# A mixture-of-experts decoder kernel in which expert gate and up rows are interleaved and loaded as pairs

## The reference

```
def swiglu(h, wg, wu, wd):
    return (jax.nn.silu(h @ wg) * (h @ wu)) @ wd

def moe_swiglu(h, router_w, wg, wu, wd):
    logits = (h @ router_w).astype(jnp.float32)
    top_val, top_idx = lax.top_k(logits, TOP_K)
    top_w = jax.nn.softmax(top_val, axis=-1)
    gates = jnp.sum(jax.nn.one_hot(top_idx, N_EXPERTS, dtype=jnp.float32) * top_w[..., None], axis=-2).astype(h.dtype)
    y = jnp.zeros_like(h)
    for e in range(N_EXPERTS):
        y = y + gates[..., e:e + 1] * swiglu(h, wg[e], wu[e], wd[e])
    return y
```

## Time and profile before

| what | value |
|---|---|
| median of three runs | 1382.75 us (1382.27 to 1382.86) |
| span of the profiled execution, first to last instruction | 1382.1 us |
| PE busy | 1368.8 us, 99% of the span |
| DVE, ACT busy | 808.3 us, 661.5 us |
| moved by DMA | 454.9 MB, 329 GB/s over the span, about 430 GB/s from 620 us to 1370 us |
| TensorE clock granted, mean | 0.998 of full speed |

### The profile page before, as it was taken

One profiled execution on the slowest core, in us unless ns is written; L12 is line 12 of the kernel. 1 busy time (PEld: TensorE's weight loads), 2 busy tenths in 40 slices (PEclk: granted clock), 3 DMA queues, 4 the chain that ended last, 5 costly groups with the idle time before them and its releaser, 6 DMA issues.

```text
span 1382.1 us, 17732 instructions
## 1 busy us (share of the span) xinstructions
PE 1368.8 (99%) x6681; PEld 938.3 (68%) x6681; DVE 808.3 (58%) x1143; ACT 661.5 (48%) x886; POOL 10.3 (1%) x22
## 2 busy tenths in 40 slices
PE   8999999999999999999999999999999999999998
PEld 7887788888898877843434888534888534888532
DVE  5878666554557786631113989423889423989311
ACT  7657646444366575511002787312787302787210
POOL 2000000000000000000000000000000000000000
PEclk9999999999999999999999999999999999999999
DMA  9555446555544576899999999999999999999997
GB/s 354 191 177 184 152 136 231 183 183 184 182 153 155 181 264 269 309 403 429 429 433 427 430 431 428 429 432 428 429 430 423 399 431 427 430 429 430 428 430 295
DMA packets 84242, 454.90 MB, mean 329 GB/s; under 512 B 5624, under 2 KB 7936, under 8 KB 58048
## 3 DMA queue, kind: packets, MB, share of 16 engines
q1 hardware_dynamic: 83232, 452.47, 81.7%
q0 software_dynamic: 752, 1.23, 0.3%
q10 hardware_dynamic: 176, 0.07, 0.0%
HBM read 452.69 MB, written 1.06 MB: 328 GB/s over the span
## 4 chain that ended last, share of the span: by engine, by line
PE 92%; DVE 3%; ACT 3%; DMA 2%; issue 1%; DVEq 0%; ACTq 0%; SPq 0%
PE pA L837 39%; PE pB L837 19%; PE pB L1351 10%; PE pA L1351 8%; PE pA L1415 7%; PE pA L861 2%; DMA first_run<-expert_w_gate_dram 2%; PE pB L861 1%; DVE w_lo L1873 1%; PE pB L1249 1%; ACT w_hi L1514 1%; PE pA L1279 0%; PE pB L1069 0%; ACT early_hi L1514 0%; DMA aqk<-mix_norm_g_dram 0%
## 5 line engine op out<-in xcount | busy, mean ns | idle before, releaser
L1873 DVE TENSOR_TENSOR w_lo<-raw,w_hi 128x1024 fp32r<-128x1024 f32 x128 | 153.1, 1220 | 58.0 <-ACT w_hi L1514 57.6
L1873 DVE TENSOR_TENSOR w_lo<-first_run,w_hi 128x1024 fp32r<-128x1024 f32 x126 | 149.1, 1219 | 30.9 <-ACT w_hi L1514 29.6
L1514 ACT ACTIVATE w_hi<-raw 128x1024 fp32r<-128x1024 f32 x128 | 131.9, 1058 | 56.2 <-PE pB L837 32.2
L1873 DVE TENSOR_TENSOR w_lo<-late,w_hi 128x1024 fp32r<-128x1024 f32 x126 | 150.8, 1222 | 11.9 <-ACT w_hi L1514 3.6
L1514 ACT ACTIVATE w_hi<-first_run 128x1024 fp32r<-128x1024 f32 x126 | 130.9, 1065 | 52.0 <-DMA first_run<-expert_w_gate_dram 26.5
L1514 ACT ACTIVATE w_hi<-late 128x1024 fp32r<-128x1024 f32 x126 | 131.8, 1060 | 30.6 <-PE pA L837 15.1
L1824 ACT ACTIVATE ex_act<-pA 64x512 f32<-64x512 f32 x15 | 8.9, 591 | 242.0 <-PE pA L1351 194.4
L1873 DVE TENSOR_TENSOR early_lo<-raw,early_hi 128x1024 fp32r<-128x1024 f32 x58 | 69.8, 1221 | 34.3 <-ACT early_hi L1514 34.2
L2373 DVE TENSOR_TENSOR x<-pA,x 128x512 f32<-128x512 f32 x28 | 18.8, 688 | 118.2 <-PE pA L1280 116.9
L1351 PE MATMUL pB<-late,x_narrow 128*64 128x512 f32 x272 | 78.0, 592 | 0.0
L837 PE MATMUL pA<-w_hi,hT_hi 128*128 128x512 f32 x192 | 77.1, 402 | 0.0
(11 more groups left out here) (463 smaller groups left out, 2792.8 us busy)
## 6 DMA issues: line engine op xcount, KB each, us to landing
first_run<-expert_w_gate_dram SPq DMA_DIRECT2D x28, 1792.0 KB, 17.7
first_run<-expert_w_up_dram SPq DMA_DIRECT2D x28, 1792.0 KB, 15.3
late<-expert_w_gate_dram SPq DMA_DIRECT2D x28, 1792.0 KB, 15.5
late<-expert_w_up_dram SPq DMA_DIRECT2D x28, 1792.0 KB, 17.4
raw<-w_in_dram SPq DMA_DIRECT2D x43, 1024.0 KB, 5.1
first_run<-expert_w_down_dram SPq DMA_DIRECT2D x21, 2048.0 KB, 15.9
late<-expert_w_down_dram SPq DMA_DIRECT2D x28, 1024.0 KB, 17.6
late<-expert_w_down_dram SPq DMA_DIRECT2D x14, 2048.0 KB, 21.9
```

The costliest lines, as they stand in the source:

```text
L1514: f(like_raw(m, halves_slot(m)[0]), raw_slot(m), ACT.Copy).then_inc(s["w_hi_done"], 1)
L1873: tt(like_raw(m, lo), raw_slot(m), like_raw(m, hi.bitcast(F32)), ALU.subtract).then_inc(s["w_lo_done"], 1)
```

## The change

The function that launches the kernel joins the gate and up matrices along their last axis before the launch, so that in DRAM each gate line of 14,336 bytes is followed by the up line of the same number. A narrow job loads such a pair of rows at once: 28,672 bytes per partition, 3.67 MB, into the place of two rows. A wide job still loads single rows, which are now every other 14,336 bytes of the joined matrix. Job 0 also reads its pieces out of the joined matrix, in the same sizes as before.

```
     def wait_item(eng, narrow, kind, c, w):
-            at_pass, run, slot = item_at[narrow][kind, c]
-            if slot == RUN_ROWS:
+            at_pass, run, slot = item_at[narrow]["gate" if narrow and kind == "up" else kind, c]
+            if slot % 2 and slot < RUN_ROWS:
+                eng.wait_ge(row_loaded[run][slot], 16 * (1 if narrow else at_pass + 2) + 64 * w)
+            elif slot == RUN_ROWS:
...
-                gate, up, down = [w[0][bass.ds(e, 1)] for w in (expert_gate, expert_up, expert_down)]
-                gate, up = [w.rearrange("e (k p) n -> p (e k) n", p=P) for w in (gate, up)]
+                both, down = [w[0][bass.ds(e, 1)] for w in (expert_gate_up, expert_down)]
+                both = both.rearrange("e (k p) n -> p (e k) n", p=P)
+                gate, up = both[:, :, 0:ROW], both[:, :, ROW:]
...
                     for (kind, c, *n), at_pass, run, slot, at, size in items[is_narrow(j)]:
+                        if is_narrow(j) and kind == "up":
+                            continue
+                        if is_narrow(j) and kind == "gate":
+                            size = 2 * ROW
                         part_free(j, at_pass, run, at, size)
-                        if kind == "down":
+                        if is_narrow(j) and kind == "gate":
+                            src = both[:, c:c + 1, :]
+                        elif kind == "down":
...
+def rows_together(gate, up):
+    import numpy as np
+    return np.concatenate([gate, up], axis=3)
```

More of the change, by code:

```diff
@@ L166, in program @@
             q_norm_g, k_norm_g, w_branch_a, w_branch_b, w_out, ffn_norm_g, dense_gate, dense_up, dense_down,
-            router_w, expert_gate, expert_up, expert_down, consts, bucket_hot, bucket_mask, bias_rows, out):
+            router_w, expert_gate_up, expert_down, consts, bucket_hot, bucket_mask, bias_rows, out):
     with ExitStack() as ctx:
@@ L2513, in tables @@
     return c.reshape(P, 8 * P), hot, mask
+def rows_together(gate, up):
+    import numpy as np
+    return np.concatenate([gate, up], axis=3)
 _INS = ["x", "rel_bias", "mix_norm_g", "w_in", "conv_w", "conv_b", "igate_b", "fgate_b", "mlstm_norm_g",
         "q_norm_g", "k_norm_g", "w_branch_a", "w_branch_b", "w_out", "ffn_norm_g", "dense_w_gate", "dense_w_up",
-        "dense_w_down", "router_w", "expert_w_gate", "expert_w_up", "expert_w_down"]
+        "dense_w_down", "router_w", "expert_w_gate_up", "expert_w_down"]
 def kernel(**inputs):
@@ L2526 @@
     nc = bacc.Bacc("TRN2", target_bir_lowering=False, num_devices=1, dynamic_dma_scratch_size=4096)
+    inputs["expert_w_gate_up"] = rows_together(np.asarray(inputs["expert_w_gate"]), np.asarray(inputs["expert_w_up"]))
     arrays = {f"{n}_dram": np.ascontiguousarray(inputs[n]) for n in _INS}
```

## The result

| | before | after |
|---|---|---|
| median | 1382.8 us (1382.27 to 1383.39) | 1389.4 us (1386.95 to 1392.29) |
| ratio | 1 | 1.0043, 95% interval 1.0032 to 1.0055 |
| span of the profiled execution | 1382.1 us | 1388.2 us |

The account below looks back on a forecast made before the run. PE was taken to set the pace, hiding the loads. 1382.1 + 0 (loads) + 0 (issue) + 0 (gate rows) = 1382.1, and with 0.65 us from span to median 1382.7 us; range 1380.9 to 1386.0 us, 8 in 10.

Parts of the forecast that it names:

- What bounds the kernel: Whole kernel: PE sets the pace and the loads keep up, with 0.8 to 1.7 us to spare.
- four places where the loads could stop PE: Starts of first, second and third wide jobs and the last load: 0.95, 1.6, 0.84 and 1.7 us to spare.
- Fewer loads, longer rows: Narrow jobs from job 1: 32 pairs replace 64 loads, -0.3 us for the stream, zero for the total.
- Later issue: Pairs issued where up rows were: job 1 loses nothing, job 5 0 to 1.0 us, taken 0.5; total zero, worst 0.2.
- The upper bound: Lead needed by a load, at most 2.7 us: a 1 MB load landed after 5.1 us, 2.4 of it moving.
- loses nothing by either: Pair 4 of job 1, lead 2.9 us: no loss by the bounds of 1.5 and 2.7 us on the lead needed.
- pairs are issued too late: Narrow jobs: queue runs dry once per job; with a need of 5 us, 6.5 us slower, 1389.2 us; chance 0.10.
- Later landing of gate rows: Narrow jobs: PE's gate row waits for its up row too; nothing lost, smallest spare 1.5 us.
- the rest: Wide jobs' doubled row spacing, SP's extra address instruction per up load, job 0's pieces, unchanged engine order: zero cost.
- Faster, by an earlier start of the second wide job: PE's wait there is the loads' after all; up to 3.5 us gained, 1379.2 us; chance 0.08.
- Slower by instruction fetches behind longer rows: Four narrow jobs: some 11 fetches each wait 0.53 us for one row more; 5.8 us, 1388.5 us; chance 0.04.

Follow-up runs that it names:

- The kernel with the shorter stream: Changed kernel, but a narrow job's load of down unit 12 brings 64 numbers per partition instead of 2048, with wrong weights there: 1384.78 us, ratio 1.0010.
- the ample kernel: Changed kernel with pairs only for rows 1, 5, 6 and 7 of each narrow job, the other rows loaded singly: 1383.03 us, ratio 1.0003.
- the first kernel of loads alone: No computation, ten phases of 14 loads with varied row bytes and loads under way: 431 GB/s at 28,672 bytes and two, 356 at 10,240 and two.
- the last kernel: Loads only, 28,672-byte rows alternating with shorter ones, second half with extra rows on ScalarE's queue: at 4.25 to 4.3 us lead, mean loss 0.0, then 0.2 us.
- the layout alone: Changed kernel with the joined matrix kept, but narrow jobs loading single rows of 14,336 bytes, each with its own wait: 1384.19 us, ratio 1.0001.
- single rows issued late: Kernel before, with two matrices, but a narrow job's gate row also waits for the place of its up row: 1389.44 us, ratio 1.0039.
- the short kernel: Changed kernel with pairs only for rows 0, 2, 3 and 4 of each narrow job, the other rows loaded singly: 1390.07 us, ratio 1.0049.

## Why the prediction was wrong, point by point

*What bounds the kernel* was right: PE sets the pace, the loads have 0.8 to 1.7 us to spare at the starts of wide jobs and at the end, and "a gain in the loads is worth nothing; a loss beyond about 0.8 us is paid". The kernel with the shorter stream shows it from the other side. But its four places where the loads could stop PE left out the last up rows of wide jobs, where 0.73 and 1.51 us of the waits stand.

*Fewer loads, longer rows* was right: 433 GB/s for pairs at ample lead against 430 expected, worth nothing in the ample kernel. In these traces a fixed cost per load shows only on an idle queue. In the first kernel of loads alone, these two, issued at 288.89 and 582.07 us, were each the first of a phase (DMA view: size and us to landing):

```profile
place<-expert_w_gate_up_dram SPq DMA_DIRECT2D x1, 1792.0 KB, 7.1
...
place<-expert_w_gate_up_dram SPq DMA_DIRECT2D x1, 3584.0 KB, 11.0
```

That is 7.1 - 4.3 = 2.8 and 11.0 - 8.5 = 2.5 us beyond the moving. The Trainium skill's page "DMA: Bandwidth & Descriptors" (section "Anatomy of one DMA") gives about 2.0 us for the GpSimd path, near these two of SP's queue; for loads behind a queue with enough work, which came 8.5 us apart for 8.5 us of moving, the trace still disagrees.

*Later issue* is the step that failed. The issues came where it put them (670.77 and 680.65 us, against 670.87 and 680.75 for the up rows), and the leads were no shorter than it had worked out (3.5 us for pair 4 of job 1 where it said 2.9, 3.0 for pair 2 of job 5 where it said 1.7). It looked at these two pairs alone, and the second lost nothing; pair 3 of job 1, which it did not look at, lost 1.4 us. What failed is the bound on the lead that is needed: 1.5 to 2.7 us, where the runs show some 4 to 5. The upper bound came from a load on a half idle queue, and the idle queue above confirms it as the time for starting and reporting there. But it is not the need of a queue that must not run dry, and "loses nothing by either" did not follow. One part of the difference is seen in the trace after: lead was counted to the landing of the load ahead, which is when the last of the 16 engines is done. Of the load ahead of pair 3 the first engine raised the semaphore at 672.45 and the last at 674.26 us, 1.8 us apart, and 672 to 676 us is where the rate falls to 320 GB/s. The Trainium skill says on the same page (section "Why a DMA increments its semaphore by 16 and not by 1") that the engines of a DMA finish independently and the semaphore counts them; the trace agrees, with that 1.8 us.

The other part is seen in the single transfers of the trace, one per row and engine: a load just issued does not reach all engines at once. From 672.15 to 673.55 us only 9 to 15 of the 16 engines had one under way, so it was 2.8 us after the issue of pair 3 that all worked again, and the first rows on five of them then took 1.7 to 2.3 us, where a row takes 1.06. Behind the issues of pair 4 in job 1 and of the last kernel's load at 211.85 us (lead 3.67) all 16 worked again after 3.5 and 3.9 us; at leads of 4.3 us in its half without extra rows they worked without a break. Behind the issues at 645.08, 870.46 and 1077.71 us, whose pairs lost nothing, it was 2.3, 2.4 and 1.2 us. Why some engines begin so late, and why the first rows take longer, stays open.

The trace of before held the answer. The prediction read the 401 GB/s of the earlier trace rows as proof that PE doesn't notice a dip, and did not ask for the cause. Two loads of job 5 in the kernel before, issued at 1076.95 and 1083.02 us, in the DMA view:

```profile
late<-expert_w_up_dram SPq DMA_DIRECT2D x1, 1792.0 KB, 10.4
...
late<-expert_w_gate_dram SPq DMA_DIRECT2D x1, 1792.0 KB, 9.9
```

And the window around the second issue, in the kernel before:

```profile
1080.00:1086.00 6.00, 6.00 (x29) 4.94 (x27) 5.20 (x5) 3.54 (x4) 0.00 (x0) 1.00 0.91 346
```

The first landed at 1087.35, so the second had 4.3 us of lead, and it landed at 1092.9, 5.5 us later instead of 4.27, with the rate at 346 GB/s. A lead of 4.3 us already lost 1.3 us there, well above the bound taken from the earlier trace rows, and for most of the 4 us behind its issue only 10 to 15 of the engines had a row under way.

*The rival "pairs are issued too late"* came true, at 1389.4 us against the 1389.2 it was priced at with a need of 5 us. Part of that agreement is chance. It counted one dry queue per narrow job, where two pairs lost in each of them. It charged 1.2 us of wait at the first wide job, where 0.87 + 0.73 were paid, and 2.5 at the third, where 1.25 + 1.51 were paid, but for a loss in job 5, whose loads were no slower than before (419 and 416 GB/s): the 2.8 us by which DVE was late there had come about by the second wide job (2.7). And the row behind the 1.51 us landed 1.7 us late with a lead of 19.8 us, beside an instruction fetch, so that wait is not due to the pairs alone. It also charged 2.8 us for a lower clock, which did not come in the profiled run (its mean granted clock was 0.999, before 0.998), and left out the end, where 0.38 + 1.20 us were paid. Its chance of 0.10 was too low, since it hung on a bound read from a load in another situation.

*Later landing of gate rows* and *the rest* were right: 80 of 80 us of PE in every narrow job, and ratio 1.0001 for the layout alone. *Faster, by an earlier start of the second wide job* was rightly set low: its first piece came 2.7 us later and the wait did not change, so it is the branch's, which took 5.95 us (row of PE's loop, in ns):

```profile
L1493 PEldq COMPARE_BRANCH  x2: 83/3014/5946, 962.3 to 1169.6; - x2
```

*Slower by instruction fetches behind longer rows* did not come: the ample kernel has 16 pairs and loses nothing, and single rows issued late lose all.

## What to carry to other kernels

Joining two loads moves the issue of the first to where the second was, and what that costs is read from the lead, from an issue to the landing of the load ahead; here loads with less than some 4 to 5 us of it landed up to 2.4 us late, though not each time. Look in the trace of before for the loads that already have the shortest leads, and for dips in the rate beside them, before taking a bound from elsewhere. Loads that are hidden behind PE can lose time as long as they have some to spare: make the sum of losses up to each place where a fresh job takes the data, and compare it with the spare time there.

## What the hardware showed unexpectedly

Behind PE's wait at the loop's branch the granted clock is lower in some runs and not in others. From 966 to 972 us it was 0.72 in the kernel before, with the joined matrix and single rows, and with single rows issued late; that is part of the time at 1.2 instead of 2.4 GHz. In the kernels after, ample, and with the shorter stream it was 1.00 (and 1.00 from 960 to 990 us), behind idle times of PE of 2.1 to 2.7 us in all six. In the short kernel it was 1.00 there, and 0.72 from 1174 to 1180 us behind another wait of 2 us. Of the kernel after:

```profile
966.00:970.00 4.00, 1.89 (x9) 1.05 (x6) 3.45 (x3) 2.67 (x3) 0.00 (x0) 1.00 1.02 434
```

The earlier trace rows has 0.65 for the same 4 us. A wait of this length thus costs some 6 x 0.28 = 1.7 us more or doesn't (an estimate from these windows), and one profile of one kernel can't tell which. The runs show that it varies from one execution of a kernel to the next: of the ample kernel's eleven, six took 1382.5 to 1383.0 us with a mean granted clock of 0.999, and five 1384.9 to 1386.6 us with 0.998; the profile is of one of the six. That the clock is all of their difference is not shown.
